# Four extra 128x128 products per half level, and one PSUM bank for both products of a level, in the delta rule's triangular inverse

## The reference

```
a_low = where(strict, beta_i * (k_i . k_j) * decay_ij, 0)
sol   = triangular_solve(I + a_low, [beta*v, beta*exp(gcum)*k])   # u, w
step(S):  v_new = u - w @ S
          o     = (q*exp(gcum)) @ S + attn @ v_new
          S     = S * exp(g_end) + kd^T @ v_new
```

## Time and profile before

| what | value |
|---|---|
| median of 3 runs | 3735.92 us |
| lowest, highest | 3731.45, 3738.05 us |
| the profiled execution's own time | 3741.29 us |
| its span, first to last instruction | 3739.4 us |
| TensorE busy | 3607.2 us (96%) |
| mean granted TensorE clock | 0.961 |
| delta rule stages | some 172 and 176 us |

### The profile page before, as it was taken

The page is one execution under the profiler, slowest core; times in us unless marked ns, Lnnn a source line. Parts: engine busy times, 40 slices in busy tenths (PEclk is TensorE's granted clock), DMA queues, the critical chain, the costliest instruction groups (busy, mean ns, idle before and its releaser), DMA issues. The chain is left out here.

```text
span 3739.4 us, 56724 instructions
## 1 busy us (share of the span) xinstructions
PE 3607.2 (96%) x23733; PEld 2997.3 (80%) x23733; DVE 1794.2 (48%) x2521; ACT 1202.7 (32%) x1842; POOL 133.7 (4%) x218
## 2 busy tenths in 40 slices
PE   8899999999999999999999999999999999999998
PEld 8758999986888886877778788878687777878887
DVE  6565524346534344356554643343435655463334
ACT  3353212235322244233342321224423334232222
POOL 0000000000000010000200100000000010010000
PEclk9999999999999999999779999999999977999999
DMA  3101222212222220221002222222022100212222
GB/s 128 58 2 68 96 86 89 91 57 60 94 97 101 79 78 35 90 91 68 2 20 100 79 98 99 87 87 79 35 82 98 57 3 32 100 68 99 102 91 92
DMA packets 49944, 278.74 MB, mean 75 GB/s; under 512 B 10238, under 2 KB 12926, under 8 KB 20539
## 3 DMA queue, kind: packets, MB, share of 16 engines
q1 hardware_dynamic: 48684, 274.29, 20.7%
q10 hardware_dynamic: 1038, 1.26, 0.1%
HBM read 273.28 MB, written 2.22 MB: 74 GB/s over the span
## 5 line engine op out<-in xcount | busy, mean ns | idle before, releaser
L447 PE MATMUL ps<-xs,ffn_w 128*128 128x512 f32 x2112 | 482.6, 390 | 6.2 <-ACT xs L302 3.5
L447 PEld LDWEIGHTS ps<-xs,ffn_w 128*128 128x128 f32 x2112 | 395.6, 188 | 92.4 <-issue 6.6
L447 PE MATMUL ps<-u,mlp_w 128*128 128x264 f32 (+1 forms) x2880 | 454.3, 320 | 0.0
L447 PEld LDWEIGHTS ps<-u,mlp_w 128*128 128x128 f32 x2880 | 415.6, 189 | 37.7
L447 PE MATMUL ps<-hn,mlp_w 128*128 128x264 f32 (+1 forms) x2304 | 363.6, 320 | 0.0
L447 PEld LDWEIGHTS ps<-hn,mlp_w 128*128 128x128 f32 x2304 | 332.4, 188 | 30.4 <-issue 0.5
L447 PE MATMUL ps<-xs,cv_w 128*128 128x512 f32 x1152 | 268.7, 393 | 0.0
L447 PEld LDWEIGHTS ps<-xs,cv_w 128*128 128x128 f32 x1152 | 214.9, 188 | 59.8 <-issue 13.7
L447 PE MATMUL ps<-ff,ffn_w 128*128 128x512 f32 x1056 | 241.1, 390 | 0.0
L447 PEld LDWEIGHTS ps<-ff,ffn_w 128*128 128x128 f32 x1056 | 198.2, 188 | 41.9 <-issue 1.0
L563 ACT CAST ffn_w<-raw 128x2048 fp32r<-128x2048 f32 (+1 forms) x74 | 124.2, 1678 | 304.0 <-PE ps L447 264.0
(11 more groups left out here) (458 smaller groups left out, 4915.6 us busy)
## 6 DMA issues: line engine op xcount, KB each, us to landing
raw<-in_w_ffn_up SPq DMA_DIRECT2D x44, 1024.0 KB, 4.8
raw<-in_w_up SPq DMA_DIRECT2D x32, 1024.0 KB, 4.8
raw<-in_w_down SPq DMA_DIRECT2D x32, 1024.0 KB, 4.8
raw<-in_w_conv SPq DMA_DIRECT2D x24, 1024.0 KB, 4.8
raw<-in_w_ffn_down SPq DMA_DIRECT2D x32, 704.0 KB, 4.1
raw<-in_w_mqk SPq DMA_DIRECT2D x10, 1024.0 KB, 4.9
raw<-in_w_qk_even SPq DMA_DIRECT2D x9, 1024.0 KB, 4.8
raw<-in_w_mv SPq DMA_DIRECT2D x8, 1024.0 KB, 4.8
```

What stands on the lines that cost most here:

```text
L447: ins = nc.tensor.matmul(bank(u)[:, h, :], w[:, s, wp, k * g.bw + j * P:k * g.bw + (j + 1) * P], g.xs[:, xp, k, h * n:(h + 1) * n], start= ...
```

## The change

At levels 2 to 6 four `keep_busy` products are put ahead of the applies, into bank 2 of head 0 (ps[:, 2]), and four at the end of the level, into bank 2 of head 1 (ps[:, 6]). So that these banks are free during the levels, W moves from bank 2 to bank 0 of its head, where Y is too: at levels 1 to 5 to other columns than Y (part 1 and, for the block that VectorE reads at level 5, part 2), at level 6 to the other half of the partitions. `quarter` takes its output always in bank 0. The wait for `u_side` moves from level 6's apply to its update, since that update writes over columns that ScalarE's `sides` reads. No product of the computation is added or removed.

```
--- before.py
+++ after.py
@@ -2575,10 +2575,10 @@
 
                 def quarter(e, b, lhs, rhs, sem):
 
-                    rows = slice(0, HC) if b == 0 else slice(HC, CHUNK)
-                    to = slice(HC, CHUNK) if b == 0 else slice(0, HC)
+                    rows = slice(HC, CHUNK) if b else slice(0, HC)
+                    to = slice(0, HC) if b else slice(HC, CHUNK)
                     for c in range(NCH):
-                        ins = nc.tensor.matmul(bank(e, b)[to, c, rows], lhs(rows, c), rhs(rows, c), start=True, stop=True)
+                        ins = nc.tensor.matmul(bank(e, 0)[to, c, rows], lhs(rows, c), rhs(rows, c), start=True, stop=True)
                     ins.then_inc(sem, 1)
 
                 def turn(e, b, data, sem):
@@ -2614,6 +2614,7 @@
                     else:
                         pe.wait_ge(s["t_cut"], i + 1)
                         pe.wait_ge(s["t_done"], i + 1)
+                        pe.wait_ge(s["u_side"], i + 1)
                         quarter(e, 0, lambda r, c: n[r, c, HC:CHUNK], lambda r, c: f["ty"][r, c, :], s["y_filled"])
 
                 def apply(i, b, e, f, s):
@@ -2623,18 +2624,17 @@
                     if b == 1 and i:
                         pe.wait_ge(s["s_done"], (NCH - 1) * i)
                     if b < small:
-                        in_blocks(e, 2, 0, yc, ut[:, 0, :, :]).then_inc(s["w_filled"], 1)
+                        in_blocks(e, 0, 1, yc, ut[:, 0, :, :]).then_inc(s["w_filled"], 1)
                     elif b == small:
                         for c in range(NCH):
                             for q, to in ((quads[1], quads[0]), (quads[3], quads[2])):
-                                nc.tensor.matmul(blocks(e, 2)[to, c, :], yc[q, c, :], ut[q, 0, c, :], start=True, stop=True)
+                                nc.tensor.matmul(blocks(e, 0, 1)[to, c, :], yc[q, c, :], ut[q, 0, c, :], start=True, stop=True)
                         for c in range(NCH):
-                            ins = nc.tensor.matmul(blocks(e, 2, 1)[quads[1], c, :], ut[quads[1], 0, c, :], yc[quads[1], c, :], start=True, stop=True)
+                            ins = nc.tensor.matmul(blocks(e, 0, 2)[quads[1], c, :], ut[quads[1], 0, c, :], yc[quads[1], c, :], start=True, stop=True)
                         ins.then_inc(s["w_filled"], 1)
                     else:
                         pe.wait_ge(s["u_cut"], i + 1)
-                        pe.wait_ge(s["u_side"], i + 1)
-                        quarter(e, 2, lambda r, c: f["ty"][r, c, :], lambda r, c: f["u"][r, c, r], s["w_filled"])
+                        quarter(e, 1, lambda r, c: f["ty"][r, c, :], lambda r, c: f["u"][r, c, r], s["w_filled"])
 
                 def aside(i, b, e, f, s):
 
@@ -2679,9 +2679,13 @@
                         for e, f, s in both:
                             update(i, b, e, f, s)
                         aside(i, b, *both[0])
+                        if b > 1:
+                            keep_busy(nc, ps[:, 2, :], ident, 4)
                         for e, f, s in both:
                             apply(i, b, e, f, s)
                         aside(i, b, *both[1])
+                        if b > 1:
+                            keep_busy(nc, ps[:, 6, :], ident, 4)
                         if i and b == 1:
                             for e, f, s in both:
                                 pick_squares(i - 1, e, f, s)
@@ -2750,7 +2754,7 @@
                     act.wait_ge(s["w_filled"], (levels - 1) * i + small)
                     act.wait_ge(s["zeros_set"], 1)
                     for q, to in ((quads[0], quads[1]), (quads[2], quads[3])):
-                        ins = nc.scalar.mul(f["u"][q, :, to], blocks(e, 2)[q, :, :], -1.0)
+                        ins = nc.scalar.mul(f["u"][q, :, to], blocks(e, 0, 1)[q, :, :], -1.0)
                     ins.then_inc(s["u_side"], 1)
 
                 def outputs(i):
@@ -2840,14 +2844,14 @@
                     dve.wait_ge(s["w_filled"], (levels - 1) * i + b)
                     if b < small:
                         ut = f["ut"][i % 2]
-                        nc.vector.tensor_tensor(ut[:, 0, :, :], ut[:, 0, :, :], blocks(e, 2), ALU.subtract).then_inc(s["first_done"], 1)
+                        nc.vector.tensor_tensor(ut[:, 0, :, :], ut[:, 0, :, :], blocks(e, 0, 1), ALU.subtract).then_inc(s["first_done"], 1)
                         dve.wait_ge(s["first_done"], small * i + b + 1)
                         nc.vector.transpose(ut[:, 1, :, :].rearrange("p c n -> p (c n)"),
                                             ut[:, 0, :, :].rearrange("p c n -> p (c n)")).then_inc(s["ut_done"], 1)
                     elif b == small:
-                        nc.vector.tensor_scalar(f["ty"][quads[1], :, 0:HB], blocks(e, 2, 1)[quads[1], :, :], -1.0, None, ALU.mult).then_inc(s["t_done"], 1)
+                        nc.vector.tensor_scalar(f["ty"][quads[1], :, 0:HB], blocks(e, 0, 2)[quads[1], :, :], -1.0, None, ALU.mult).then_inc(s["t_done"], 1)
                     else:
-                        nc.vector.tensor_scalar(f["u"][0:HC, :, HC:CHUNK], bank(e, 2)[0:HC, :, HC:CHUNK], -1.0, None, ALU.mult).then_inc(s["u_done"], 1)
+                        nc.vector.tensor_scalar(f["u"][0:HC, :, HC:CHUNK], bank(e, 0)[0:HC, :, HC:CHUNK], -1.0, None, ALU.mult).then_inc(s["u_done"], 1)
 
                 def add_squares(i, e, f, s):
                     dve.wait_ge(s["picked"], i + 1)
```

## The result

The changed kernel takes 3751.34 us (median of 6 runs, 3746.88 to 3753.73), the kernel before, beside it, 3732.15 (3730.12 to 3738.05). The ratio is 1.0048, 95% interval 1.0037 to 1.0058: half a per cent slower.

What follows compares the result with a forecast made beforehand. TensorE's instruction queue was taken to bound the two delta-rule stages, over half their time at half clock. Layer losses of 4.0 and 3.1 us made +7.1: 3748.4 for the profiled execution, 3743.0 for the median, range 3729 to 3757.

Steps and rivals of the forecast that it cites:

- 0.93 or more: Windows over the two delta-rule stages: granted clock was to rise to this from 0.75 and 0.73.
- The group, sized at 0.97: Four added products in TensorE's queue: 0.97 us at full clock; 80 groups, 77.6 us.
- Level 6, sized by halving: Pair 1's 64x64 products: 3.46 us at half clock, 1.73 at full, 3.67 with groups.
- The 4.05 of pair 0: Level 3 at full clock in pair 0, taken as basis for level 3 with groups: 6.00 us.
- The last pair: Pair 3: levels 2 to 6 and w_turned 20.4 us, 1.4 more; 0.6 comes back behind; loses 0.8.
- Pair 0 of layer 2: Groups lift the clock during level 2, one running at half: 43.9 us against 43.49, loses 0.4.
- its base: Profiled execution 3741.3 us lay 5.4 above the median 3735.9, so 3748.4 became 3743.0 for the median.
- Rival 1: Groups don't hold the clock in the delta stages: about 15.5 us a pair, near 120 in all, 3856; chance 0.05.
- Rival 2: Clock mostly holds, may fall in level 3 or stay slow in pair 0: +13 us, 3756; chance 0.25.
- Rival 3: Faster: groups partly fall into TensorE's waits, deciding once one costs under 0.78 us net: 3727.8; chance 0.14.
- Its other leg: Small products at full clock run twice as fast, not 1.5 times: 0.4 us a pair.
- Rival 4: Moved wait for u_side shows: 0.8 us in two pairs or some 2 in all, 3745 to 3758; chance 0.06.

Runs made afterwards that it cites:

- e1: The changed kernel without both groups of added products, keeping W in bank 0 and the moved wait: 3735.35 us, ratio 1.0001 to the kernel before.
- e3: The changed kernel with eight products in each group instead of four: 3826.79 us in one execution.
- e4: The changed kernel with each group's four 128x128 products replaced by four of 8 rows by 512 columns: 3874.8 us in one execution.
- e2: The changed kernel with two products in each group instead of four: 3732.64 us, ratio 1.0000 to the kernel before, two far slower executions left out.
- e5: The changed kernel with two products in each group and no groups in the last pair: 3735.36 us, ratio 1.0005 to the kernel before.
- e10: The changed kernel with only one group of four at the end of levels 2, 3 and 4, in pairs 0 to 2: 3714.31 us, ratio 0.9951.
- e7: The changed kernel without the groups ahead of the applies, four products kept at the end of levels 2 to 6: 3724.60 us, ratio 0.9978.
- e11: The changed kernel without the groups at the levels' ends, the four products ahead of the applies kept: 3736.81 us, ratio 1.0006.
- e6: The changed kernel with groups only in levels 3 (three, three), 4 (two, two) and 6 (two), pairs 0 to 2: 3736.42 us, ratio 1.0015.
- e8: The changed kernel with groups of four kept but none in the last pair: 3745.5 us in one execution.

## Why the prediction was right, and which terms were off

**The mechanism held, step by step.** From the first group of pair 0 to the stage's end the clock stayed at 2.4 GHz, in both layers; it reads 0.95 where 0.93 or more was named. A group takes its whole time in TensorE's queue, less the waits that it covers. e1 shows that bank and wait add nothing that can be measured, e3 that the price follows the number of products, so the loss is what the groups cost less what the clock gives back. In pair 2, in us, measured against predicted:

| | predicted | measured |
|---|---|---|
| level 1 | 4.35 | 4.36 |
| level 2 | 6.12 | 6.35 |
| level 3 | 6.00 | 5.78 |
| level 4 | 3.32 | 3.55 |
| level 5 | 5.29 | 5.42 |
| level 6 | 3.67 | 4.22 |
| w_turned | 1.79 | 1.79 |
| recurrence | 9.65 | 9.65 |
| pair | 40.2 | 41.1 |

**The group, sized at 0.97, costs 1.09 between small tiles.** The prediction took a value between 0.89 (full products on both sides) and 1.05, and 1.09 lies outside: the way out of small tiles and back is 0.20 us. With full products on one side, as in level 5 and ahead of w_turned, a group takes 0.99. The 0.12 over the estimate, in the two groups of a level, is nearly all of the 0.23 that levels 2 and 4 are over. In level 5 (pair 1, 1851.41 to 1856.84) the full products, the kernel's own and the added, took 3.97, not 3.72, and the small ones 1.46, not 1.57.

**Level 6, sized by halving, was too short.** Its sets of 64x64 products were 1.73 at half clock and are 1.07 at full (1897.95 to 1899.02), not 0.87: a factor 0.62. This is the largest miss within the pair, 0.55.

**Level 3 came out 0.22 below, for a wait was taken for work.** The 4.05 of pair 0 on which it was built (1798.40 to 1802.45) has this in it:

```profile
1799.99 0.72 PE L2591 MATMUL ps<-rows,sel 8*128 8x512 f32 x2 [0.18 <-DVE qkv L2796]
```

The two spreads of the first half there take 1.55 from start to start (1799.09 to 1800.64), and those of the second half 1.12. In the changed kernel both halves take 1.12 or 1.11 (1883.89 to 1885.01, 1886.78 to 1887.89): the spreads no longer wait for VectorE. That gives 0.43 back, against 0.24 by which the two groups cost more than 1.94.

**A stall came that was not foreseen.** Pair 1 of layer 1 has a wait in level 1 that no release explains:

```profile
1832.69 0.33 PE L2586 MATMUL ps<-mats,qkv 128*128 128x128 f32 x1
1833.84 0.49 PE L2586 MATMUL ps<-mats,qkv 128*128 128x128 f32 x3 [0.81 <-issue]
```

Its level 1 took 5.33 instead of 4.36. The stall of 1.16 in before's last pair is gone: such stalls move from place to place, and cannot be counted on in a sum.

**The last pair lost 1.8 and 1.6 instead of 0.8.** In layer 1 its levels 2 to 6 and w_turned take 21.07 (1917.96 to 1939.03) where 20.4 was added up, by the prices of the groups and of level 6. And behind w_turned 0.3 came back, not 0.6: the first products of the recurrence end earlier, but the next one then waits 0.40 for ScalarE (at 1940.03).

**Pair 0 of layer 2 gained instead of losing 0.4.** Its start, beside the earlier trace rows:

```profile
3001.26 0.66 PE L2573 MATMUL ps<-delta_ut,delta_nb 32*32 32x32 f32 x32 [4.95 <-DVE delta_ut L2840]
...
3005.99 1.08 PE L2573 MATMUL ps<-delta_ut,delta_nb 32*32 32x32 f32 x64
...
3008.36 1.16 PE L102 MATMUL ps<-mats 128*128 128x128 f32 x8
...
3012.46 0.75 PE L2573 MATMUL ps<-delta_ut,delta_nb 32*32 32x32 f32 x64
```

The clock was up before the first group (1.16, not 2.08), so levels 1 and 2 took 11.20 with two groups in them where they had taken 11.23 with none; the prediction had 14.2. The rest of the pair took 30.4 where 29.7 was predicted. The rise stands ahead of every group of the pair, so it isn't their doing: e1, with none, took 40.34 for this pair, before 43.49. Where the clock rises in pair 0 differs by some 3 us between kernels with the same work there, and a forecast can't name it. Here it was luck: with the 0.4 us of loss that was predicted for this pair the forecast would have been 2.3 us further off. By pairs the sum is 2.2 + 3.2 + 1.1 + 1.8 in layer 1 and -1.9 + 2.5 + 1.1 + 1.6 in layer 2: 11.6 us where +7.1 was predicted, and 12.0 the measured difference of the two executions. That makes 4.9 of the 8.3 us by which the forecast fell short. The other 3.5 are its base: it took 5.4 off for the way from a profiled execution to the median, and for the changed kernel that way was 1.9.

**The rivals.** Rival 1 (the groups don't hold the clock) is refuted by the clock itself, and e4 shows that what spoke for it, a full queue at half clock, was no evidence: with 8-row products in the place of the 128-row ones the queue was as full and the clock stayed down. Rival 2 (it holds mostly) did not occur with four products, but it is just what two products do (e2, e5). Rival 3 (faster) needed a group below 0.78 net of the waits that it covers. A group takes 1.09, and the pairs at full clock tell the net price: 34.41 with three groups (e10), 36.08 with five at the levels' ends (e7), 37.41 with five ahead of the applies (e11), 41.11 with all ten. Five front groups added to e7's cost 1.01 each; five end groups added to e11's cost 0.74 each. So the rival was right that groups fall in part into waits, and wrong in how much: by the sum over the pairs a group still cost more than the clock gave back. Its other leg, small products twice as fast at full clock, is wrong: 0.75 against 1.08 recorded, 0.68 against 1.01 from start to start (1791.42 to 1792.43 in the changed kernel, still at half clock). Rival 4 (the moved wait shows) is real only without the group: 0.37 us in e1's last pair, and no wait on that instruction in the changed kernel, where it is L2757.

**Where the gain went.** Holding the clock, with the waits that are covered, gives a pair some 8 us: 38.55 before, plus seven groups at 1.09 and three at 0.99, less 41.11. The change pays 10.6 for it, in ten groups. e10 pays three groups, some 3.3 us, keeps most of the gain, and pays nothing in the last pair: 18 groups in the kernel, not 80. That explains why the same idea is 0.5% slower here and 0.5% faster there.

## What to carry to other kernels

Products added to hold TensorE's clock cost nearly their whole time when its queue sets the time, so price them first: sum what the stretch would take at full clock, and divide the difference by the cost of a group, the way out of small tiles and back included. Then put few groups of four rather than many of two (e7 against e2), where TensorE would wait anyway (e7 against e11), and in the levels in which the clock falls and the one before them: e6, without groups in level 2, lost the clock at the start of level 3, while e10, with groups in levels 2 to 4 alone, was the fastest. In the last pair groups were not worth their price (e8, one execution). Time several places: the same four products a level gave 0.9978 at the level's end and 1.0006 in its middle. A busy TensorE is no sign of a full clock; read the granted clock of the stretch.

## What the runs showed of the hardware that was not expected

- TensorE busy in 38.00 of 38 us ran at 0.50 of its clock (e4), with 8-row and 32x32 products for the most part, and with 64x64 and some full ones. With groups of four full-array products in the place of the 8-row ones it ran at 1.00, busy in 17.00 of 17 us.
- From half to full clock a set of 64 products of 32x32 goes from 1.01 to 0.68 us from start to start, a factor of 0.67. Four full 128x128 products between small tiles go from 2.00 to 1.09, 0.55. So part of the time of the 32x32 sets did not shrink with the clock. For 16 products of 64x64 it is 1.73 to 1.07, 0.62; but between the groups of e4 such a set took 1.90 at half clock (1883.52 to 1885.42), which would make it 0.56, so for these it is open.
- Leaving the small tiles for the whole array and coming back costs 0.20 us, whatever number of products is between (2, 4 and 8 measured).
- Waits of up to 1.8 us with no release in the trace appear within dense runs of small products and move from one pair to another between kernels (1.16 and 1.47 before, 0.81 after, 0.73 and 0.67 in e2, 1.76 in e5). Their cause stays open.
